# Block-diagonal delta levels: 128x128 products against two 64x64 tiles with sums kept in PSUM

## The reference

```python
def gated_delta_chunked(q, k, v, g, beta, s0):      # chunks of 64 tokens
    gc = jnp.cumsum(g, axis=-1)
    kb = k * beta[..., None]; vb = v * beta[..., None]
    decay = jnp.exp(jnp.where(tri, gc[..., :, None] - gc[..., None, :], -jnp.inf))
    lower = jnp.where(strict, jnp.einsum('bhncd,bhnsd->bhncs', kb, k) * decay, 0.0)
    t_inv = triangular_solve(lower + eye, eye)      # (I + lower)^-1
    u = t_inv @ vb
    w = t_inv @ (kb * jnp.exp(gc)[..., None])
    ...
o_f, s_f = gated_delta_chunked(q, k, v, g[:, :, 0], beta[:, :, 0], s0[:, 0])
o_b, s_b = gated_delta_chunked(flip(q), flip(k), flip(v), flip(g[:, :, 1]), flip(beta[:, :, 1]), s0[:, 1])
```

## Time and profile before

| | before |
|---|---|
| median of 3 runs | 1075.55 us (1074.47 to 1089.63) |
| the profiled execution | 1074.91 us, its span 1073.1 us |
| granted TensorE clock over the span | 0.971 |
| busy, PE / PEld / DVE / ACT / POOL | 967.0 / 554.4 / 343.9 / 232.6 / 151.7 us |
| DMA | 299.50 MB, 279 GB/s in the mean |
| instructions | 13951, of them 5486 matmul passes |

### The profile page before, as it was taken

One profiled execution on the slowest core, in us unless ns is written; L12 is line 12 of the kernel. 1 busy time (PEld: TensorE's weight loads), 2 busy tenths in 40 slices (PEclk: granted clock), 3 DMA queues, 4 the chain that ended last, 5 costly groups with the idle time before them and its releaser, 6 DMA issues. The chain is left out here.

```text
span 1073.1 us, 13951 instructions
## 1 busy us (share of the span) xinstructions
PE 967.0 (90%) x5486; PEld 554.4 (52%) x5486; DVE 343.9 (32%) x814; ACT 232.6 (22%) x573; POOL 151.7 (14%) x161
## 2 busy tenths in 40 slices
PE   7799989898979798999999999889898979899896
PEld 3344456664323332347787667768785323333333
DVE  1101116248101110124343676578528401111015
ACT  2110046131201010123233421213513201001013
POOL 1100000011000000001000166567111000000000
PEclk9899999799999999999999899999998989999999
DMA  9996792065999999997664500222234699999992
GB/s 385 421 381 247 292 350 103 1 227 206 400 429 429 426 426 429 428 424 331 228 242 163 230 1 1 79 78 79 79 119 195 268 407 423 426 428 427 426 426 103
DMA packets 23308, 299.50 MB, mean 279 GB/s; under 512 B 2688, under 2 KB 2816, under 8 KB 5440
## 3 DMA queue, kind: packets, MB, share of 16 engines
q1 hardware_dynamic: 21744, 292.45, 66.5%
q0 software_dynamic: 1488, 6.03, 1.5%
HBM read 295.32 MB, written 3.15 MB: 278 GB/s over the span
## 5 line engine op out<-in xcount | busy, mean ns | idle before, releaser
L628 PE MATMUL bank<-ring,arena 128*32 128x512 f32 (+1 forms) x1216 | 201.2, 601 | 11.9 <-DMA ring<-slots 11.9
L628 PEld LDWEIGHTS bank<-ring,arena 128*32 128x32 f32 (+1 forms) x1216 | 61.6, 124 | 146.9 <-issue 134.7
L651 PE MATMUL bank<-ring,arena 128*32 128x512 f32 (+1 forms) x608 | 105.3, 618 | 27.4 <-DMA ring<-slots 21.8
L907 DVE TENSOR_TENSOR arena<-arena,bank 128x256 f32<-128x256 f32 x28 | 11.8, 421 | 302.3 <-ACT arena L736 302.3
L1666 PE MATMUL bank<-ring,act_t 128*128 128x512 f32 x192 | 88.2, 613 | 3.8 <-DVE act_t L1931 3.0
L1066 PE MATMUL bank<-act_t,ring 128*128 128x256 f32 x384 | 89.5, 388 | 0.4 <-DVE act_t L491 0.4
L1066 PEld LDWEIGHTS bank<-act_t,ring 128*128 128x128 f32 x384 | 72.5, 194 | 14.5 <-issue 4.2
L651 PEld LDWEIGHTS bank<-ring,arena 128*32 128x32 f32 (+1 forms) x608 | 29.8, 126 | 84.7 <-issue 70.6
L974 POOL COPY arena<-arena 128x512 f32 (+1 forms) x34 | 17.6, 517 | 386.5 <-PE bank L628 307.8
L1666 PEld LDWEIGHTS bank<-ring,act_t 128*128 128x128 f32 x192 | 36.5, 196 | 51.5 <-issue 46.1
L991 PE MATMUL bank<-act_t,ring 128*128 128x256 f32 x256 | 60.3, 400 | 1.6 <-ACT act_t L1895 0.8
(11 more groups left out here) (335 smaller groups left out, 1278.9 us busy)
## 6 DMA issues: line engine op xcount, KB each, us to landing
ring<-slots SPq DMA_DIRECT2D x136, 2048.0 KB, 12.6
ring<-slots SPq DMA_DIRECT2D x8, 512.0 KB, 9.5
cst<-consts SPq DMA_DIRECT2D x1, 1260.5 KB, 37.0
act_t<-x_t POOLq DMA_DIRECT2D x1, 1024.0 KB, 11.7
ring<-state POOLq DMA_DIRECT2D x1, 1024.0 KB, 5.3
out_st<-arena POOLq DMA_DIRECT2D x4, 256.0 KB, 2.8
out_y<-arena SPq DMA_DIRECT2D x4, 256.0 KB, 2.1
par<-params SPq DMA_DIRECT2D x1, 613.0 KB, 4.0
```

The source lines that it names most:

```text
L628: last = pe.matmul(bk[to:to + wide, :], x[:, 4 * m + c, wide * e:wide * e + wide], w[:, c, 512 * t:512 * t + 512], start=(m == 0 and c == ...
L651: last = pe.matmul(bank[3][to:to + wide, :], ht[:, col + wide * e:col + wide * e + wide], w[:, f, 512 * t:512 * t + 512], start=(f == 0), ...
```

## The change

The levels below the last join blocks within tokens 0 to 63 or within 64 to 127, so everything in them lies in two diagonal blocks of 64x64. The change works on these alone.

- Each product of levels 1 to 5 becomes two on 64x64 tiles: b = 0 on rows and columns 0 to 63 of the array, b = 1 on 64 to 127 (`middle_products`, `outer_products`).
- X and XT are no longer summed in SBUF. `first_blocks` writes the identity and level 0 for both of them side by side into bank 4u+2 by products with the identity, and the outer products of the levels add to it there. After each level DVE reads the bank once and writes X and XT, both masked, to SBUF (`masked_pair`, 512 columns for a set).
- The middle products take ACT's copy of LT's diagonal blocks (LT64), masked by POOL (LM64); all of Y, LM and LT have 256 columns a set.
- The last level makes the two off-diagonal blocks, one for each direction (`last_products`). ACT copies the forward one (`forward_corner`) and DVE the backward one next to the diagonal blocks (`merged`). `new_values` is split into a part that needs only a diagonal block (64x64 tiles) and a part on 128x64 tiles.
- The masks `level` and `half` shrink from 13 x 128 to 13 x 64 columns of the constants, which a DMA brings in at the beginning.
- POOL's identity sum, its masks of XT and its last mask go; so do ACT's copy of X and DVE's sums.

```diff
@@ delta_pe
+            def new_values(s, u): ...
+                for j in range(4):
+                    for d in range(2):
+                        pe.matmul(bank[4 * u + 2 * s + d][rows64[d], j * P:(j + 1) * P], merge[2][rows64[d], j, :],
+                                  rhs(d, j, rows64[d]), start=True, stop=True)
                 pe.wait_ge(S("xt_forward"), 2 * s + u + 1)
                 pe.wait_ge(S("xt_backward"), 2 * s + u + 1)
+                for j in range(4):
+                    for d in range(2):
+                        last = pe.matmul(bank[4 * u + 2 * s + d][rows64[1 - d], j * P:(j + 1) * P], merge[d][:, j, :],
+                                         rhs(d, j, slice(0, P)), start=True, stop=True)
+            def first_blocks(s, u):
+                eye = [ident[rows64[b], 64 * b:64 * b + 64] for b in range(2)]
+                for b in range(2):
+                    pe.matmul(bk[rows64[b], :].rearrange("p (h n) -> p h n", h=8), eye[b],
+                              eye[b].unsqueeze(1).to_broadcast([64, 8, 64]), start=True, stop=False, skip_group_check=True)
+                for b in range(2):
+                    pe.matmul(bk[rows64[b], 256:512], eye[b], w["XT0"][rows64[b]].rearrange("p h n -> p (h n)"),
+                              start=False, stop=True, skip_group_check=True)
+                for j in range(4):
+                    for b in range(2):
+                        last = pe.matmul(block64(bk, b, j), w["XT0"][rows64[b], j, :], eye[b], start=False, stop=True, ...)
+            def middle_products(s, lv, u):
+                for j in range(4):
+                    for b in range(2):
+                            last = pe.matmul(block64(bank[4 * u], b, j), w["LM64"][rows64[b], j, :], w["X64"][rows64[b], j, :],
+                                             start=True, stop=True)
+            def outer_products(s, lv, u):
+                pe.wait_ge(S("ly_copied"), lev(s, lv, u))
+                for j in range(4):
+                    for b in range(2):
+                        pe.matmul(block64(bank[4 * u + 2], b, j), w["XT64"][r, j, :], w["Y64"][r, j, :],
+                                  start=False, stop=True, skip_group_check=True)
+                        last = pe.matmul(block64(bank[4 * u + 2], b, j, 1), w["Y64"][r, j, :], w["XT64"][r, j, :],
+                                         start=False, stop=True, skip_group_check=True)
...
-                    transposes(pe, bank[4 * u], [sets[u]["XT"][:, j, :] for j in range(4)]).then_inc(S("x0_done"), 1)
+                    first_blocks(s, u)
...
+                for u in range(2):
+                    last_products(s, u)
+                    if s == 1:
+                        pe.wait_ge(S("xn_ready"), 3 + u)
+                        state_products(u, 1, 4 * u + 2)
@@ delta_pool
-                    pool.tensor_tensor(w["XT"], w["XT"], mask4(ident), ALU.add).then_inc(S("xt0_ready"), 1)
...
+                        pool.tensor_tensor(w["LM64"], w["LT64"], mask64("level", lv), ALU.mult).then_inc(S("lm_ready"), 1)
@@ delta_dve
-                    dve.tensor_tensor(decay[s][:, u, 0], sets[u]["X"], level_mask("half", 1), ALU.mult)\
-                        .then_inc(S("xm_ready"), 1)
+                def masked_pair(u, lv):
+                    dve.tensor_tensor(sets[u]["XM"], bank[4 * u + 2][:, :].rearrange("p (h n) -> p h n", h=8),
+                                      mask64("half", lv - 1, 8), ALU.mult).then_inc(S("xm_ready"), 1)
...
+                        for b in range(2):
+                            r = rows64[b]
+                            dve.tensor_tensor(merged[s][u][1 - b][r], halves64(u, 1)[r], mask64("half", lv, 4, r), ALU.mult)\
+                                .then_inc(S("w_ready"), 1)
+                    if lv == LEVELS - 2:
+                        for u in range(2):
+                            dve.tensor_tensor(merged[s][u][2], halves64(u, 1), mask64("half", lv + 1), ALU.mult)\
+                                .then_inc(S("xn_ready"), 1)
```

More of the change, by code:

```diff
@@ L124, in build_program @@
         ident = c_("ident")
+        masks = cst[:, CONST_W["level"][0]:CONST_W["level"][0] + 512]
         sems = {}
@@ L378, in keep_busy @@
             for _ in range(n):
-                pe.matmul(bk[:, :], ident, c_("level")[:, 0:512], start=True, stop=True)
+                pe.matmul(bk[:, :], ident, masks, start=True, stop=True)
         def ln_pe(pe, site):
@@ L1131, in new_values, with last_products @@
+            def last_products(s, u):
+                w = sets[u]
+                pe.wait_ge(S("ly_copied"), lev(s, LEVELS - 1, u))
+                pe.wait_ge(S("w_ready"), 4 * s + 2 * u + 2)
+                for j in range(4):
+                    for b in range(2):
+                        r = rows64[1 - b]
+                        last = pe.matmul(block64(bank[4 * u + 1 - b], b, j), w["Y64"][r, j, :], merged[s][u][b][r, j, :],
                                          start=True, stop=True)
-                last.then_inc(S("vn_done"), 1)
+                last.then_inc(S("dx_done"), 1)
@@ L1181, in delta_pe @@
                     for u in range(2):
-                        w = sets[u]
-                        pe.wait_ge(S("lm_ready"), lev(s, lv, u))
-                        pe.wait_ge(S("xm_ready"), lev(s, lv, u))
-                        for j in range(4):
-                            last = pe.matmul(bank[4 * u][:, j * P:(j + 1) * P], w["LM"][:, j, :], decay[s][:, u, 0, j, :],
-                                             start=True, stop=True)
-                        last.then_inc(S("ly_done"), 1)
@@ L1341, in delta_act @@
                 for u in range(2):
-                    act.wait_ge(S("x0_done"), 2 * s + u + 1)
-                    act.activation(sets[u]["X"], heads4(bank[4 * u][:, :]), ACT.Copy).then_inc(S("x0_copied"), 1)
+                    w = sets[u]
+                    act.wait_ge(S("lt_masked"), 4 * s + 2 * u + 2)
+                    for b in range(2):
+                        last = act.activation(w["LT64"][rows64[b]], w["LT"][rows64[b], :, 64 * b:64 * b + 64], ACT.Copy)
+                    last.then_inc(S("lt_copied"), 1)
                 gate_copy(2 * s)
@@ L1353, in delta_act, with forward_corner @@
                         out_rms(0)
+                def forward_corner(u):
+                    act.wait_ge(S("dx_done"), lev(s, LEVELS - 1, u))
+                    act.activation(merged[s][u][0][rows64[0]], bank[4 * u + 1][rows64[0], 0:256].rearrange("p (h n) -> p h n", h=4),
+                                   ACT.Copy).then_inc(S("xt_forward"), 1)
+                if s == 0:
+                    for u in range(2):
+                        forward_corner(u)
                 if s == 0:
```

173 lines of the change are left out of this document (90 added, 83 removed).

## The result

The changed kernel takes 1048.09 us in the median of 4 runs (1045.34 to 1049.3), beside 1078.14 us for the kernel before in the same measurement. The ratio is 0.97 with a 95% interval of 0.9622 to 0.9779. The forecast was 1050.0 us.

What follows compares the result with a forecast made beforehand. It took PE to bound levels 2 to 5. Gains of 12.8 us (s=0) and 13.7 (s=1), together 26.5, less 1.7 for half clock, left 24.8: 1074.9 to 1050.1 us; forecast's own range 1043 to 1056, overall 1042 to 1068.

Steps and rivals of the forecast that it cites:

- Levels 2 to 5: Delta stage levels 2 to 5: 5.3 us a level against 7.35, gaining 8.2 us in s=0 and 8.4 in s=1.
- The pass at 0.030: 64x64 products: 0.030 us for a 64-column pass if two tiles overlap, 0.060 if one follows the other.
- the change of tiling at 0.2: PE switching between tile shapes: 0.19 us a change, two changes a level put at 0.4 us.
- The wait for ACT's copy: Levels 2 to 5, before set 0's outer products: PE waits 0.2 us, 0.3 with the first pass after it.
- PE bounds the levels: Levels 2 to 5 before the change: PE busy 29.10 of 29.40 us; the other engines fit in 5.3 us a level.
- Starts: Start and level 1 of each token half: gain 0.2 us in s=0 and 5.1 in s=1, 1.7 of it half clock.
- Tails: After the levels: s=0 from 11.5 to 7.1 us, gain 4.4; s=1 to 19.4, gain 0.2, from -2 to +2.
- one more half-clock stretch: Gaps in the tail of s=0 could bring PE to half clock once more: 1.7 us taken off the gain.
- The tiles take turns: Rival, every 64x64 product: a pass at 0.060 us, a level 7.9 us, total 1088 us; chance 0.10.
- The chain is longer: Rival, levels 2 to 5: longer hand-overs or delayed masks make a level 6.2 us, total 1057 us; chance 0.22.
- The clock falls: Rival, levels 2 to 5: PE granted half the clock, 37 us more, total 1086 us; chance 0.06.

Runs made afterwards that it cites:

- one product more: Changed kernel with one more 512-column product behind the gate passes of each of levels 2 to 5: level 6.00 us against 5.14, 1056.84 us, ratio to before 0.9808.
- tiles only: Kernel before with only the products of levels 1 to 5 on 64x64 tiles, plus zeroing products; other engines' operations unchanged: 1074.48 us beside 1079.3, ratio 0.9938.
- sums in PSUM only: Kernel before with X and XT summed in PSUM and masked from there by DVE, products still 128x128: level 7.13 us, ratio to before 1.004.
- the bare level: Changed kernel with the gate's second half moved into levels 2 and 3, levels 4 and 5 without gate passes: such a level 3.44 us; ratio to before 0.9715.

## Why the prediction was right

**Levels 2 to 5.** The forecast was 5.3 us a level, measured 5.14. The pass at 0.030 (0.029 measured) and the change of tiling at 0.2 held. The wait for ACT's copy was put at 0.3 us and came out at 0.2: the last middle pass and the first outer one start 0.236 apart (642.897 and 643.133), where passes come every 0.029. Gain in both halves 8.8 and 9.0 where I had 8.2 and 8.4.

**The bound.** "PE bounds the levels" held before and holds after: one product more costs all of itself. What the prediction did not say is how near the other bound was. With tiles alone levels 3 and 4 take 6.65 us, so the lighter work of DVE, POOL and ACT, of which I only said that it fits in, is worth more than half of the gain there (1.5 of 2.2 us). How much of that is the sums in PSUM and how much the narrower operations wasn't measured.

**Starts.** s=0: gain 0.2 expected, 0.5 measured: gates and first blocks took 10.96 us to the first middle products, not 11.4, since the first blocks took 2.09 and 1.99 us with their changes of tiling and not 2.2; DVE's mask came 1.06 later, not 0.9. s=1: 5.1 expected, 5.5 measured, with a wait of 0.89 us for the masks of level 1.

**Tails.** s=0: 7.1 expected, 7.0 measured, the new values of both sets 4.1 (663.62 to 667.71) where I had 4.2. s=1: 0.2 expected, 0.2 to 0.6 measured.

**Sum and the clock.** The stage gained 28.8 where the steps gave 26.5. The 1.7 us that I took off for one more half-clock stretch did not come in the stage; its granted clock is 1.00 throughout. The 1.7 us that I counted as gained in the start of s=1 did come. The kernel before did 3.24 us of work at half clock there (1.2 GHz), behind a stretch in which PE was busy 1.13 of 3.40 us:

```profile
705.00:708.40 3.40, 1.13 (x8) 0.97 (x8) 3.40 (x3) 0.91 (x3) 3.40 (x3) 1.00 0.85 265
708.40:711.80 3.40, 3.24 (x15) 3.27 (x16) 0.01 (x1) 0.84 (x2) 3.40 (x3) 0.50 0.82 352
```

Both kernels that keep PE's waits there have such a stretch at the same place (tiles only 0.57 from 706.4 to 710.0 us, sums in PSUM only 0.52 from 711.5 to 715.0), and in both executions of the changed kernel the stage keeps 1.00 throughout; so this part belongs to the change, and not to the scatter of the clock.

That the total came so near is in part luck. The forecast started from the profiled execution of the kernel before, 1074.91 us, and the median of the four runs is 1078.14: by the medians the change is worth 30.1 us, 5.3 more than the 24.8 forecast. By the profiled executions it is 25.6, since the changed kernel's lost 3.3 us ahead of the stage, in which the change has no part. In the stage alone the steps were 2.3 us too low.

**The tiles take turns.** Refuted. The two tiles of a pair write one bank at once at 0.029 us a pass, and with one tile the same passes cost 0.058, a level of 7.65 us where the rival had 7.9. The Trainium skill, "TensorEngine Tiling (Array Packing)", section "Restrictions and Gotchas", says that different row tiles can't access one bank at the same time. By that the level would have been about what the single tile gave; it was 5.14, with the two tiles in different rows and different columns of the array, so in different partitions of the bank. Row tiles that write the same partitions of one bank were not tried.

**The chain is longer.** Refuted: the bare level is 3.44 us, and a chain of 6.2 would have shown there. The chance of 0.22 that I gave it was too much; the idle time of DVE and POOL in the old rows already spoke against it.

**The clock falls.** It didn't: 1.00 in both stretches of levels.

## What to carry to other kernels

When a stage is bound by one engine at nearly its whole length, ask what the second engine would make of the stage if the first were halved; here both had to be relieved: the smaller tiles alone gave 0.7 to 1.1 of 2.2 us a level, and the sums in PSUM alone 0.2. Two 64x64 tiles on the diagonal gave twice the passes only where the code alternates between them in short runs: up to four passes of one tile in a row were free, and with sixteen the outer products took 60% more. And read an edit of a few us from its own stretch, since the totals of one and the same kernel were 6 us apart in two measurements, with its stage the same to 0.1 us.

## What was not expected of the hardware

- The other tile's run begins only when about three passes of the present one are left: runs of 16, 8 and 4 passes of 64 columns on one tile cost 0.047, 0.036 and 0.029 us a pass.
- A start flag reaches beyond what its product writes. With start=True on every 64-column product of a bank, behind the product of 256 columns that wrote the bank's other half, the outputs behind the delta stage were wrong. With start=True on the product of 256 columns alone, one for each 64 partitions, and on none of the others they were right; so those found nothing old in their own columns. That the first terms were overwritten is inferred from this, and the sums themselves were not read. The Trainium skill, "PSUM — Partial Sum Buffer", section "The four PSUM rules", says that a start marks the whole bank of the written partitions as unwritten and that the next product without a start overwrites there. The two kernels agree with it.
- Rows of a pass say 0.22 us for 64 columns whether one tile works or two: only the distance between starts shows that they overlap.
- The stretches at half clock lay elsewhere in each execution ahead of and behind the stage, with no product changed there: 621 to 634 us up to the stage, 306 to 312 behind it. Within the stage, in the start of s=1, one came back at the same place in all three kernels that keep PE's waits there.
